# Sixteen more tokens take fetched expert rows in the down projection, with a shorter top-k and decode

## What is computed

```python
def peer(h, w_query, sub_keys, expert_down, expert_up):       # 8 heads, 128 sub-keys, top 16
    q = (h @ w_query).reshape(B, S, PEER_HEADS, 2, half)
    s1 = jnp.einsum('bshd,kd->bshk', q[..., 0, :], sk[0])
    s2 = jnp.einsum('bshd,kd->bshk', q[..., 1, :], sk[1])
    v1, i1 = lax.top_k(s1, PEER_TOPK)
    v2, i2 = lax.top_k(s2, PEER_TOPK)
    cand = (v1[..., :, None] + v2[..., None, :])               # 16 x 16 sums
    cand_idx = (i1[..., :, None] * N_KEYS + i2[..., None, :])
    top_s, top_pos = lax.top_k(cand, PEER_TOPK)
    expert_idx = jnp.take_along_axis(cand_idx, top_pos, axis=-1)
    gates = jax.nn.softmax(top_s, axis=-1)
    ...                                                        # per token, 8 * 16 = 128 experts e:
    act = jax.nn.gelu(jnp.einsum('td,ted->te', hx, expert_down[idx]))
    return jnp.einsum('te,ted->td', act * g, expert_up[idx])
```

## Time and profile before

| | |
|---|---|
| median of 3 runs | 2019.37 us (2018.9 to 2020.83) |
| the profiled execution | 2019.42 us |
| its span, first to last instruction | 2017.6 us |
| TensorE / VectorE / GpSimd / ScalarE busy | 99% / 68% / 59% / 40% of the span |
| mean granted TensorE clock | 0.997 |

### The profile page before, as it was taken

One profiled execution on the slowest core, in us unless ns is written; L12 is line 12 of the kernel. 1 busy time (PEld: TensorE's weight loads), 2 busy tenths in 40 slices (PEclk: granted clock), 3 DMA queues, 4 the chain that ended last, 5 costly groups with the idle time before them and its releaser, 6 DMA issues.

```text
span 2017.6 us, 28859 instructions
## 1 busy us (share of the span) xinstructions
PE 1991.7 (99%) x10179; PEld 1759.8 (87%) x10179; DVE 1372.8 (68%) x2244; ACT 803.9 (40%) x1077; POOL 1198.3 (59%) x650
## 2 busy tenths in 40 slices
PE   7999999999999999999999999999999999999997
PEld 6888888887888888999999999999888888888886
DVE  6424242333722399899997878783797889888946
ACT  5222222233633343333334656565434333333353
POOL 5342424243245244888887655555899888888821
PEclk9999999999999999999999999999999999999998
DMA  6231313233233322889998888888999999999911
GB/s 213 74 113 63 115 60 113 68 120 95 74 94 106 114 84 86 306 294 321 320 323 313 292 305 302 297 303 300 336 386 384 369 363 354 361 372 362 361 64 42
DMA packets 167334, 455.00 MB, mean 226 GB/s; under 512 B 13264, under 2 KB 62416, under 8 KB 165456
## 3 DMA queue, kind: packets, MB, share of 16 engines
q1 hardware_dynamic: 58032, 209.04, 30.9%
q0 software_dynamic: 36864, 134.23, 17.2%
q10 hardware_dynamic: 72352, 110.64, 16.0%
HBM read 396.71 MB, written 54.53 MB: 224 GB/s over the span
## 4 chain that ended last, share of the span: by engine, by line
PE 95%; DVE 2%; ACT 1%; DMA 1%; ACTq 0%; issue 0%; SPq 0%; DVEq 0%
PE bank L861 29%; PE bank L863 29%; PE bank L862 29%; PE bank L1103 4%; PE bank L969 1%; PE bank L1052 1%; PE bank L1037 1%; PE bank L1013 0%; PE bank L1023 0%; DMA xT<-x_cols 0%; DVE bank L1266 0%; ACTq L736 0%; PE bank L938 0%; DVE h_lo L1274 0%; PE bank L926 0%
## 5 line engine op out<-in xcount | busy, mean ns | idle before, releaser
L455 POOL TENSOR_TENSOR w_lo<-raw,w_hi 128x1024 fp32r<-128x1024 f32 x390 | 937.9, 2412 | 707.3 <-ACT w_hi L501 704.0
L861 PE MATMUL bank<-h_hi,w_hi 128*128 128x384 f32 (+2 forms) x1560 | 560.8, 359 | 0.2 <-ACT scr L706 0.2
L863 PE MATMUL bank<-h_hi,w_lo 128*128 128x384 f32 (+2 forms) x1560 | 549.4, 352 | 0.0
L862 PE MATMUL bank<-h_lo,w_hi 128*128 128x384 f32 (+2 forms) x1560 | 549.0, 352 | 0.0
L501 ACT ACTIVATE w_hi<-raw 128x1024 fp32r<-128x1024 f32 x390 | 407.5, 1057 | 178.3 <-PE bank L863 61.6
L863 PEld LDWEIGHTS bank<-h_hi,w_lo 128*128 128x128 f32 x1560 | 293.0, 188 | 20.6
L861 PEld LDWEIGHTS bank<-h_hi,w_hi 128*128 128x128 f32 x1560 | 293.4, 188 | 20.0 <-issue 0.5
L862 PEld LDWEIGHTS bank<-h_lo,w_hi 128*128 128x128 f32 x1560 | 293.5, 188 | 19.7
L863 PE MATMUL bank<-w_hi,b_lo 128*128 128x512 f32 x768 | 298.8, 389 | 0.0
L862 PE MATMUL bank<-w_lo,b_hi 128*128 128x512 f32 x768 | 298.8, 389 | 0.0
L861 PE MATMUL bank<-w_hi,b_hi 128*128 128x512 f32 x768 | 298.8, 389 | 0.0
(11 more groups left out here) (190 smaller groups left out, 2547.4 us busy)
## 6 DMA issues: line engine op xcount, KB each, us to landing
raw<-weights SPq DMA_DIRECT2D x390, 512.0 KB
act_scratch<-scr ACTq DMA_DIRECT2D x64, 384.0 KB
gate_scratch<-scr ACTq DMA_DIRECT2D x12, 2048.0 KB
scr<-gate_scratch ACTq DMA_DIRECT2D x22, 768.0 KB
scr<-act_scratch ACTq DMA_DIRECT2D x22, 768.0 KB
xT<-gate_scratch ACTq DMA_DIRECT2D x10, 768.0 KB
xT<-act_scratch ACTq DMA_DIRECT2D x10, 768.0 KB
scr<-scr ACTq DMA_DIRECT2D x20, 128.0 KB, 2.8
```

Of the source, the lines that this page charges most:

```text
L455: return nc.gpsimd.tensor_tensor(w_lo[:, s, :], raw[:, s % RAW, :], w_hi[:, s, :].bitcast(F32), ALU.subtract)
L861: nc.tensor.matmul(out, a_hi, c_hi, start=first, stop=False)
L862: nc.tensor.matmul(out, a_hi, c_lo, start=False, stop=False)
L863: return nc.tensor.matmul(out, a_lo, c_hi, start=False, stop=last)
```

## The change

Sixteen of the 384 dense tokens (368 to 383) leave the down products: `down` multiplies 368 columns (`TZ`), and their products with the 128 chosen experts come from fetched rows. The 16 tokens are copied eight times over the 128 partitions (`copies_hi`, `copies_lo`), so that one fetch serves 16 tokens with 8 experts each, and 16 more fetches and dots do it (144 in all, `NROWS`). `h_tok` is overwritten by these copies after 85 dots and by the old tokens after 101, each time by the 16 identity matmuls (`token_rows`). In the dense way the 16 tokens stay: the constant 1 stands where their activations were, and their gates are multiplied by gelu of the dots. The up stage is as it was.

The other parts: of the 256 sums only 112 are formed and searched (the first four rows whole, of the other twelve four columns each), as pair (a, b) can be among the best 16 only if (a+1)(b+1) is at most 16. Positions are turned into row and column for two heads at a time. The row's index of a fetch comes from a sum of its own ahead of the dense tokens' keys. The one-hots of a quad are one compare of 512 elements and four operations of 128 elements that compare and multiply by the gate at once. The exponential moves to unit 68, the transposes to unit 70, and the fetches and dots have new places. Eleven of the twelve groups of gates for the first two read-backs are read at unit 120, the rest at unit 123.

```diff
+NX = 16
+TZ = TD - NX
...
-SELECT_AT = 3
+EXP_AT, SELECT_AT = 4, 6
...
+WIDE_ROWS, NARROW = 4, 4
+NWIDE = WIDE_ROWS * TOPK
+NCAND = NWIDE + (TOPK - WIDE_ROWS) * NARROW
...
-DOTS_DECODE, DOTS_HEAD = 2, 13
-DOTS_EXP, DOTS_SELECT, DOTS_START = 4, 6, 4
+DOTS_DECODE, DOTS_HEAD = 2, 15
+DOTS_EXP, DOTS_SELECT = 4, 4
...
-DOT_QUADS = tuple(range(1, TG // 2, 2))
+DOT_QUADS = ((1, 3, 5, 8, 9, 11, 12, 14, 15),
+             (0, 2, 3, 5, 6, 8, 9, 11, 12, 13),
...
+NMAIN = DOTS_EARLY + 3
+NROWS = NPAIR + NX
+REP_AT, TOK_AT, EXTRA_TURN = (0, 2), (1, 7), 5
...
+FETCH_AT = (2, 2, 3, 3, 6, 7, 8, 9, 10, 10, 12, 12, 13, 14, 15, 16, 16, 18, 18, 19, 20, 22, 23, 24, 25,
...
+                    if extra:
+                        pool.wait_ge(extra_ready, 1)
+                    elif n % TOPK == 0:
...
+                    if r >= U_SLOTS:
+                        pool.wait_ge(dot_done, r - U_SLOTS + 1)
...
-                nc.scalar.activation(act[:, c % 4, :], bank[:, c % 2, 0:TD], ACT.Gelu_apprx_tanh).then_inc(act_ready, 1)
+                nc.scalar.activation(act[:, c % 4, 0:TZ], bank[:, c % 2, 0:TZ], ACT.Gelu_apprx_tanh).then_inc(act_ready, 1)
...
+                gates_back(h, slice(NTG - 1 if h < 2 else 0, NTG))
...
+                if c == EXP_AT:
                     sc.wait_ge(top_ready, 1)
...
+                    nc.scalar.activation(gates_s, bank[:, 6, 0:TD], ACT.Copy).then_inc(keysT_ready, 1)
...
+            sc.wait_ge(extra_dotted, 1)
+            nc.scalar.activation(act_extra, dots_extra, ACT.Gelu_apprx_tanh).then_inc(extra_gelu, 1)
...
-                if c == 2:
-                    for b in range(2):
-                        sc.wait_ge(gate_written[b], 16 * (NTG // 2))
+                if c == 0:
+                    sc.wait_ge(gate_written[0], 16 * (NTG // 2))
+                    sc.wait_ge(gate_written[1], 16 * (NTG // 2 - 1))
+                    for h in range(2):
+                        gates_back(h, slice(0, NTG - 1))
+                if c == 3:
+                    sc.wait_ge(gate_written[1], 16 * (NTG // 2))
                     read_back(0)
                     read_back(1)
-            sc.wait_ge(dot_done, NPAIR)
...
+            def token_rows(of):
+
+                for k in range(KT):
+                    for n, h in enumerate((h_hi, h_lo)):
+                        ins = nc.tensor.matmul(h_tok[:, P * k:P * k + P], of(h, k), ident_r[:, :],
+                                               start=n == 0, stop=n == 1)
+                ins.then_inc(htok_done, 1)
...
-                    ins = mm3(bank[:, c % 2, 0:TD], w_hi[:, s, P * k:P * k + P], w_lo[:, s, P * k:P * k + P],
-                              h_hi[:, k, 0:TD], h_lo[:, k, 0:TD], k == 0, k == KT - 1)
+                    ins = mm3(bank[:, c % 2, 0:TZ], w_hi[:, s, P * k:P * k + P], w_lo[:, s, P * k:P * k + P],
+                              h_hi[:, k, 0:TZ], h_lo[:, k, 0:TZ], k == 0, k == KT - 1)
...
+                    if isinstance(j, int) and (j, c) == REP_AT:
+                        pe.wait_ge(dot_done, NMAIN)
+                        pe.wait_ge(copies_ready, 2)
+                        token_rows(lambda h, k: (copies_hi if h is h_hi else copies_lo)[:, k, :])
+                    if isinstance(j, int) and (j, c) == TOK_AT:
+                        pe.wait_ge(dot_done, NMAIN + NX)
+                        token_rows(lambda h, k: h[:, k, TD:S])
...
+                together([lambda: ts(u[0], ps, 4, None, ALU.logical_shift_right),
+                          lambda: ts(u[1], ps, 2, None, ALU.logical_shift_right),
+                          lambda: ts(u[2], ps, TOPK - 1, None, ALU.bitwise_and),
+                          lambda: ts(u[3], ps, NARROW - 1, None, ALU.bitwise_and)])
...
+                step(nc.vector.tensor_reduce(ids_p, p3, AX_XY, ALU.add))
+                mark(nc.vector.tensor_copy(expert_of[:, at], ids_p), expert_ready)
...
+                    best([(cand[:, t, :], taken[:, t, 0:NCAND], top[:, t, h, :], pos[:, h, t, :]) for t in range(TT)],
...
+            step(stt(out=ids_extra, in0=keysT[:, 0, TZ:TD], scalar=float(NKEY), in1=keysT[:, 1, TZ:TD],
+                     op0=ALU.mult, op1=ALU.add))
+            turn(ids_extra)
+            mark(tt(expert_extra, turned[:, 0, :], turned[:, 1, :], ALU.add), extra_ready)
...
-                tt(onehot(q, slice(0, 4), slice(0, 2)), iota_p.unsqueeze(1).unsqueeze(1).to_broadcast([P, 2, 4, P]),
-                   four_keys(j, q), ALU.is_equal).then_inc(oh_compared, 1)
...
-                tt(gated[q % 4], onehot(q, slice(0, 4), 1).bitcast(F32), gate, ALU.mult).then_inc(oh_ready, 1)
...
+                tt(onehot(q, slice(0, 4)), iota_p.unsqueeze(1).to_broadcast([P, 4, P]),
+                   keys[:, 0, :].unsqueeze(2).to_broadcast([P, 4, P]), ALU.is_equal)
+                for x in range(4):
+                    ins = ts(gated[q % 4][:, x, :], iota_p, keys[:, 1, x:x + 1],
+                             gates_T[:, j, q // quads, c + x:c + x + 1], ALU.is_equal, ALU.mult)
+                ins.then_inc(oh_ready, 1)
...
+                    if done[0] == NMAIN + NX and not extras[0]:
+                        extras[0] = 1
+                        ve.wait_ge(dot_done, NMAIN + NX)
+                        turn(dots_extra)
+                        mark(tt(dots_extra, turned[:, 0, :], turned[:, 1, :], ALU.add), extra_dotted)
...
+            next_dots(NLAST)
```

More of the change, by code:

```diff
@@ L742, in gate_turn @@
                     stage_gates(j, 2 * c + 1)
-                    if c == 1 and not isinstance(j, int):
+                    if c == 1 and not (isinstance(j, int) and j == 0):
                         store_gates(j - 1, 1)
@@ L762, in _ @@
             sc.dma_start(pT[:, :, :], pT_d).then_inc(p_landed, 16)
-            with sc.Fori(1, NTG // 2) as j:
+            for j in range(1, TOK_AT[0] + 1):
+                gate_turn(j)
+            sc.wait_ge(extra_dotted, 1)
+            nc.scalar.activation(act_extra, dots_extra, ACT.Gelu_apprx_tanh).then_inc(extra_gelu, 1)
+            with sc.Fori(TOK_AT[0] + 1, NTG // 2) as j:
                 gate_turn(j)
@@ L1063, in _ @@
                     pe.wait_ge(ident_ready, 1)
-                    for k in range(KT):
-                        for n, h in enumerate((h_hi, h_lo)):
-                            ins = nc.tensor.matmul(h_tok[:, P * k:P * k + P], h[:, k, TD:S], ident_r[:, :],
-                                                   start=n == 0, stop=n == 1)
-                    ins.then_inc(htok_done, 1)
+                    token_rows(lambda h, k: h[:, k, TD:S])
                 if m == 0:
@@ L1126, in _ @@
                 down(FIRST_Z, c)
-            scatter_turn(0)
-            with pe.Fori(1, NTG // 2) as j:
+            for j in range(TOK_AT[0] + 1):
+                scatter_turn(j)
+            with pe.Fori(TOK_AT[0] + 1, NTG // 2) as j:
                 scatter_turn(j)
@@ L1550, in four_keys @@
                 c = 4 * (q % quads)
[L1551 to L1565 removed]
+                keys = keys_T[:, :, j, q // quads, c:c + 4]
@@ L1569, in one_hots @@
                 for q in range(2 * quads):
-                    if q + 1 < 2 * quads:
-                        compare(j, q + 1)
-                    elif not last:
-                        compare(j + 1, 0)
-                    times_gate(j, q)
-                    if j == 0 and q == 2:
-                        next_dots(DOTS_START)
-                    if q in DOT_QUADS:
-                        dot()
-            compare(0, 0)
+                    one_hot(j, q)
+                    next_dots(DOT_QUADS[j].count(q))
```

179 lines of the change are left out of this document (108 added, 71 removed), and 12 rows, old and new, of tables (DOT_QUADS, EARLY_FETCH, FETCH_AT).

## The result

The changed kernel takes 2007.4 us (median of four executions, 2006.7 to 2008.6) against 2020.1 us on the same chip: ratio 0.9934, interval 0.9917 to 0.9951. It is faster, by 12.7 us of the 16.4 forecast, and 4.4 us slower than the forecast of 2003.0, inside its range. The profiled execution took 2008.63 us (span 2006.8).

A forecast was written before the change was run, and what follows sets the result against it. The down stage was taken to last as long as its TensorE matmuls: -20.4 (columns) + 3.5 (token rows) + 0.5 (all six seams, from 0 to 8) = -16.4 us, from 2019.42 to 2003.0 us, range 2001.0 to 2010.0.

The forecast's parts named there:

- Columns: 20.4 us: Down stage: each of 3072 matmuls takes 6.6 ns less with 368 columns than with 384, 20.4 us less.
- (a): Rival: down columns cost less near 384, 0.31 ns each, so 15.1 us less and 2008.3 us; chance 0.04.
- (d): Rival: down matmuls of 368 columns take as long as those of 384, 2023.4 us; chance 0.02.
- Token rows: 3.5 us: Amid the scatters: `token_rows` issued twice more, 16 matmuls each, adds 3.5 us on TensorE, nothing for waits on dots.
- VectorE in the quads: Quads of the down stage: VectorE needs 2.0 to 2.4 us a quad against TensorE's 2.90, so stays ahead.
- rival (c): Quads: the four compare-and-gates wait for GpSimd, 3.36 us a quad against 2.90, 44 us over 96 quads, 2047; chance 0.04.
- Seam (1): First fetch waits for the first decode, indices 4 to 11 us later, GpSimd standing still; hidden from TensorE.
- The shorter search: VectorE before the quads: 112 sums for 256 save 24 us beside TensorE, giving nothing by itself but paying for 16 dots.
- Seams (2) to (4): Gates ready 1.3 us before transposes; first scatter late 1.3 us at worst; rows land in 7.3 us, 11 us left.
- Seam (5): End of down stage: GpSimd waits at unit 123 for eight last dots; they take 9.1 of VectorE's 17.9 us to spare.
- Seam (6): Down stage transfers rise from 309 and 295 to about 330 GB/s, against 386 reached in the up stage.
- rival (b): Waits at seams (1) to (6) and the two token rows add up to 7 us, 2009.5; chance 0.11.

The follow-up runs named there:

- the repeat: The changed kernel run again unchanged, on one chip beside other versions: 2006.1 us, ratio 0.9936 to the kernel before.
- the version with the dots sooner: Against the changed kernel, four of the eight last dots moved into the last turn of quads, their rows fetched sooner: 2001.5 us, ratio 0.9909 to the kernel before.
- the last version (256, fetch later): Changed kernel searching 256 values again, first four row fetches moved from units 2, 2, 3, 3 to 4, 4, 5, 5: 2012.7 to 2025.3 us.

## Why the prediction was right, and what it missed

The forecast's direction, its main terms and its range hold. One term doesn't, the 0.5 us for the seams, and with it one of the signs that the forecast named for itself came true: it called itself wrong if TensorE waited for more than 3 us, and TensorE waited for 3.2 in the profiled execution (3.2 in all in the repeat, 3.0 the longest).

- **Columns: 20.4 us. Right.** 166.7 ns a step, and undone they cost 20.5 less 1.2, most of it waits that shrank. Rivals (a) and (d) are out. So is the rule of the Trainium skill, "TensorE: Matmul & The Clock Gate", section "Back-to-back issue gap", by which the 16 columns would have been worth 6.4 us.
- **Token rows: 3.5 us. Right.** 1.74 us each, at 1107.27 and at 1184.29, and TensorE waited for no dot ahead of them. The chain around the first, which answers to the earlier trace rows:

```profile
1106.38 0.89 PE bank L1161 x8
1107.27 1.74 PE bank L1114 x16
1109.00 0.22 PE bank L915
```

- **VectorE in the quads: right in its end, wrong in its row.** Four gated one-hots take 1.28 us (0.32 from start to start, 0.40 long), not 0.8 to 1.1, and the quad 1.88 against 1.73 before. I had taken the nearest row, an operation of the search that reads SBUF alone. It was still under 2.90 with its dots (2.52), and the bound of rival (c) was the right one to state: where it is passed, the loss is what the sum says.

```profile
1113.20 0.69 DVE L1652 TENSOR_TENSOR b_hi<-bank,scr 128x512 fp32r<-128x512 f32 x1
1113.80 1.36 DVE L1655 TENSOR_SCALAR scr<-bank,scr 128x128 f32<-128x128 f32 x4
1115.08 0.68 DVE L1652 TENSOR_TENSOR b_hi<-bank,scr 128x512 fp32r<-128x512 f32 x1
```

- **Seam (1), the first decode: hidden, as said.** The fetch came at 800.24, at the late end of what I had (4 to 11 us behind 789.5, so 793.5 to 800.5), in an execution whose stage began 2.2 us late.

```profile
788.84 2.40 POOL L484 TENSOR_TENSOR w_lo<-raw,w_hi 128x1024 fp32r<-128x1024 f32 x1 [3.99 <-ACT w_hi L534]
800.24 1.08 POOL L508 DMA_INDIRECT xT<-peer_down,scr  x1 [9.00 <-DVE scr L1596]
```

- **The shorter search gives nothing by itself: wrong as a judgement of its worth.** It is beside TensorE in the changed kernel, but with the old length of search, and all else in its place, the gain of the columns is gone. Whether another order of the work would win it back with the old search, no run shows.
- **Seams (2) to (4): right.** The gates were ready 0.7 us ahead of the transposes (1.3 forecast), the first one-hots 1.7 us ahead of the first scatter, and no row was late for TensorE.
- **Seam (5), the last dots: wrong.** This is the step that failed. I asked only whether VectorE had time for them. It had; but the dots free the slots, so the last four rows were fetched at 1376.80 to 1385.14, into the read-backs, and a write that a gelu needed landed 17.9 us after its issue. Fetched by 1364.73, the rows cost TensorE nothing.
- **Seam (6), transfers: mis-sized.** 312 to 331 GB/s in the long stretches was as forecast (about 330). I compared a mean over 603 us with the 386 of the up stage, and took it for room; the last 43 us ran at a share of 1.00, and the queue held the engine that issued into it for 5.4 us. The mean of those 43 us is no measure either: the version with the dots sooner has the same and no wait.
- **The sum.** For all seams I took 0.5 us; they cost 3.2, and 1.4 of slow clock in the profiled execution. 620.43 - 16.4 = 604.0 for the stage, measured 607.5 and 606.1. With the fetches out of the way it is 602.45, some 1 us below the sum without any seam (603.5); where that comes from stays open. The other 2.2 us of the profiled execution are its start. That 2007.4 lies in the range owes something to rival (b), for which the range was drawn up to 2010.0. Rival (b) had 7 us of waits where 3.2 came (and 1.4 of slow clock), and it put them at the first scatter, the transposes or the identity matmuls, and the one that came stood at none of these.

## What to carry to other kernels

Ask what runs beside the one transfer that an engine waits for: a mean of 320 GB/s over a stage can hide issues that hold their engine for 5 us, and a mean over the last 43 us was the same with the wait (366 GB/s) and without it (370). Where a ring of buffers ties a fetch to the work that frees the slot, moving that work to a quiet end moves the fetch there as well. Where an engine shares its time with another, look at the longest and the mean of its rows, not at the median; here the forms with an operand in PSUM were the ones that never waited.

## What the runs showed of the hardware

A DMA's issue is no fixed cost: one write of 384 KB took 0.34 us to issue (at 1371.05, ahead of the store and the reads) and the next 5.4, behind 3.4 MB issued in the 7 us before; one read of 768 KB took 9.25; and the engine did no other work meanwhile. TensorE's clock fell to its lower level behind a wait of 3.2 us in the changed kernel (some 11 steps of 307 ns in place of 167), and not behind one of 3.0 in its repeat, nor behind one of 3.4 in the last version (256, fetch later). A multiplication of 512 elements with both inputs in SBUF took 0.69 us undisturbed and up to 3.48 beside GpSimd; with one input in PSUM it took 0.67 to 0.68. Two scalars from SBUF and 128 elements from PSUM took 0.40 us, 0.32 from start to start, in every one of 384.
